# Score, selection and recurrence products over 128 rows with zeroed halves, in place of 64- and 4-row products, in a two-block transformer kernel

## The reference

```python
s = (einsum('bqhd,bkhd->bhqk', qn, k_nope) + einsum('bqhr,bkr->bhqk', qr, k_rope)) * ATTN_SCALE
```

```python
s = einsum('bhcqd,bhckd->bhcqk', q_blk, k)          # c = 0, 1; d = 64
p = softmax(where(mask, s, -inf)); a = p[:, :, 0] - lam * p[:, :, 1]
```

```python
w = exp(D - m) * einsum('bhcjd,bhcsd->bhcjs', q, k); h = einsum(w, v) / max(|w.sum|, exp(-m))
```

## Time and profile before

| | us |
|---|---|
| median of 3 runs | 2067.62 |
| lowest, highest | 2066.59, 2071.74 |
| span of the profiled execution, first to last instruction | 2061.6 |
| TensorE busy in it | 1951.5 (95%) |
| VectorE busy | 879.3 (43%) |
| ScalarE busy | 671.9 (33%) |
| mean granted TensorE clock | 0.985 of full |

### The profile page before, as it was taken

The page is one execution under the profiler, slowest core; times in us unless marked ns, Lnnn a source line. Parts: engine busy times, 40 slices in busy tenths (PEclk is TensorE's granted clock), DMA queues, the critical chain, the costliest instruction groups (busy, mean ns, idle before and its releaser), DMA issues. The chain is left out here.

```text
span 2061.6 us, 36391 instructions
## 1 busy us (share of the span) xinstructions
PE 1951.5 (95%) x16088; PEld 1383.8 (67%) x16088; DVE 879.3 (43%) x1395; ACT 671.9 (33%) x1138; POOL 60.4 (3%) x97
## 2 busy tenths in 40 slices
PE   7999989888999999998889999999999999999998
PEld 5554444445885444444468888878888888887887
DVE  4111111104641111111156656875655665786663
ACT  2000000004440000000054546674545554675552
POOL 0000000000000000000020000010000000011000
PEclk8999999999999999999999999999999999999999
DMA  9999999998669999999966545336545555425551
GB/s 409 399 426 426 426 426 426 427 425 354 265 251 424 426 428 426 427 426 427 425 284 219 189 168 184 126 126 220 195 172 200 201 184 184 153 96 192 194 194 62
DMA packets 56767, 598.33 MB, mean 290 GB/s; under 512 B 6291, under 2 KB 6803, under 8 KB 9747
## 3 DMA queue, kind: packets, MB, share of 16 engines
q1 hardware_dynamic: 55444, 592.44, 71.9%
q10 hardware_dynamic: 1152, 3.41, 0.6%
HBM read 594.78 MB, written 1.05 MB: 289 GB/s over the span
## 5 line engine op out<-in xcount | busy, mean ns | idle before, releaser
L1978 DVE TENSOR_TENSOR SPLIT<-RING,SPLIT 128x2048 fp32r<-128x2048 f32 (+2 forms) x178 | 398.9, 2256 | 143.7 <-ACT SPLIT L1456 143.5
L758 PE MATMUL PS<-RING,WK 128*32 128x512 f32 x816 | 367.4, 604 | 41.1 <-DVE WK L2247 26.1
L1125 PE MATMUL PS<-HTB,SPLIT 128*128 128x512 f32 x1152 | 404.4, 397 | 0.0
L1456 ACT ACTIVATE SPLIT<-RING 128x2048 fp32r<-128x2048 f32 (+2 forms) x178 | 332.7, 1888 | 49.7 <-DMA RING<-in_units 49.7
L1126 PE MATMUL PS<-HTB,SPLIT 128*128 128x256 f32 x1152 | 321.4, 279 | 0.0
L758 PEld LDWEIGHTS PS<-RING,WK 128*32 128x32 f32 x816 | 86.8, 111 | 284.6 <-issue 249.6
L1125 PEld LDWEIGHTS PS<-HTB,SPLIT 128*128 128x128 f32 x1152 | 216.2, 188 | 51.7
L1604 ACT ACTIVATE WK<-PS 128x128 f32<-128x128 f32 x64 | 17.8, 278 | 691.8 <-PE PS L724 691.8
L1126 PEld LDWEIGHTS PS<-HTB,SPLIT 128*128 128x128 f32 x1152 | 216.9, 188 | 0.2
L724 PE MATMUL PS<-RING,WK 128*32 128x128 f32 x5696 | 185.7, 276 | 6.7 <-issue 6.5
L724 PEld LDWEIGHTS PS<-RING,WK 128*32 128x32 f32 x5696 | 162.2, 110 | 29.8 <-issue 27.5
(11 more groups left out here) (341 smaller groups left out, 2344.7 us busy)
## 6 DMA issues: line engine op xcount, KB each, us to landing
RING<-in_units SPq DMA_DIRECT2D x171, 1024.0 KB, 4.8
RING<-in_w_down SPq DMA_DIRECT2D x53, 2048.0 KB, 32.6
RING<-in_w_gate SPq DMA_DIRECT2D x45, 2048.0 KB, 30.6
RING<-in_w_up SPq DMA_DIRECT2D x44, 2048.0 KB, 34.1
WK<-in_w_up SPq DMA_DIRECT2D x17, 2048.0 KB, 34.6
WK<-in_w_gate SPq DMA_DIRECT2D x16, 2048.0 KB, 33.6
WK<-in_w_down SPq DMA_DIRECT2D x6, 2048.0 KB, 36.8
SEAT<-in_w_up SPq DMA_DIRECT2D x3, 2048.0 KB, 27.8
```

The lines of the kernel that those rows point to most:

```text
L758: t = pe.matmul(PS[32 * i:32 * i + 32, 4 + h, :], mo.HE[:, pb, 32 * f:32 * f + 32], v[:, c, 512 * h:512 * h + 512], start=f == 0, stop=f == 3)
L1125: pe.matmul(out.rearrange("p (z b n) -> p z b n", z=2, b=2), wh, HTB[:, :, :, c, :], start=start, stop=False)
L1456: ac.activation(unit_part(u, 0), loaded(u), ACT.Copy).then_inc(s_hi, 1)
L1978: dv.tensor_tensor(unit_part(u, 1), loaded(u), unit_part(u, 0).bitcast(F32), ALU.subtract).then_inc(s_lo, 1)
```

## The change

- `ml.KR` (256 columns) becomes `ml.KZ`, two copies of 256 columns: copy 0 has the rotated key on partitions 0 to 63 and zeros below, copy 1 the reverse. `scores(h)` takes all 128 rows of `ml.QR` and copy h mod 2.
- `mx.DK` becomes `mx.KZ`, two heads in turn, each with two such copies, for d = 0 and 1.
- `mx.MM` is cleared on all 128 partitions, and the selection product runs over 128 rows.
- The convolved queries go by silu from `mx.CO` into the halves of `mx.KZ` (which the scores have left by then), two half-row instructions for each query channel; the keys stay in place.
- POOL clears `ml.KZ` at the start of mla, and `mx.KZ` and `mx.MM` at the start of each mixer, after the previous stage's last product. VectorE waits for that.
- For keys, VectorE multiplies by the cosine in place in `TQ`, and so first waits for the swap product that reads `TQ`; then it adds twice, once per half.

```diff
-        ml.KR = al(256)
+        ml.KZ = al(512).rearrange("p (z n) -> p z n", z=2)
-        mx.DK = al(1024).rearrange("p (h n) -> p h n", h=4)
+        mx.KZ = al(1024).rearrange("p (k z n) -> p k z n", k=2, z=2)
@@ POOL, mla
+                    po.memset(ml.KZ, 0.0).then_inc(s_mh, 1)
@@ POOL, mixer
+                    po.wait_ge(s_unit, UNIT[stage])
+                    for v in (mx.KZ, mx.MM):
+                        po.memset(v, 0.0).then_inc(s_mh, 1)
@@ TensorE, mla scores
-                    pe.matmul(o, ml.QR[dp:dp + 64, pr, i * 128:i * 128 + 128], ml.KR[dp:dp + 64, 0:m], start=False,
+                    pe.matmul(o, ml.QR[:, pr, i * 128:i * 128 + 128], ml.KZ[:, h % 2, 0:m], start=False,
@@ TensorE, decays
-                pe.matmul(PS[:, 6, 0:256], cs("sel")[0:4, h * 128:h * 128 + 128], mx.MM[0:4, :], start=True, stop=True)
+                pe.matmul(PS[:, 6, 0:256], cs("sel")[:, h * 128:h * 128 + 128], mx.MM, start=True, stop=True)
...
-                    pe.wait_ge(s_cos, 4 * l + 4)
-                k, q = mx.CO[dp:dp + 64, 2 * ch + 1, :], mx.CO[dp:dp + 64, 2 * ch, :]
+                    pe.wait_ge(s_cos, 6 * l + 6)
+                k, q = mx.CO[:, 2 * ch + 1, :], mx.KZ[:, ch, h % 2, :]
@@ TensorE, differential scores
-                        t = pe.matmul(o, mx.DQ[64 * d:64 * d + 64, h, i * 128:i * 128 + 128],
-                                      mx.DK[64 * d:64 * d + 64, h, 0:128 + 128 * i], start=True, stop=True)
+                        t = pe.matmul(o, mx.DQ[:, h, i * 128:i * 128 + 128], mx.KZ[:, h % 2, d, 0:128 + 128 * i],
+                                      start=True, stop=True)
@@ ScalarE
-                    ac.activation(mx.CO[:, i, :], mx.CO[:, i, :], ACT.Silu).then_inc(s_cos, 1)
+                    if i % 2:
+                        ac.activation(mx.CO[:, i, :], mx.CO[:, i, :], ACT.Silu).then_inc(s_cos, 1)
+                        continue
+                    for z in range(2):
+                        half = slice(64 * z, 64 * z + 64)
+                        ac.activation(mx.KZ[half, i // 2, z, :], mx.CO[half, i, :], ACT.Silu).then_inc(s_cos, 1)
@@ VectorE, key of mla
-                dv.tensor_tensor(ml.KR, ml.TQ[:, 0, :], cos, ALU.mult).then_inc(own.up(), 1)
                 dv.wait_ge(s_latp, 1)
+                dv.tensor_tensor(ml.TQ[:, 0, :], ml.TQ[:, 0, :], cos, ALU.mult).then_inc(own.up(), 1)
...
-                dv.tensor_tensor(ml.KR, ml.KR, ml.R2, ALU.add).then_inc(s_latv, 1)
+                dv.wait_ge(s_mh, 2)
+                dv.tensor_tensor(ml.KZ[0:64, 0, :], ml.TQ[0:64, 0, :], ml.R2[0:64, :], ALU.add).then_inc(own.up(), 1)
+                dv.tensor_tensor(ml.KZ[64:128, 1, :], ml.TQ[64:128, 0, :], ml.R2[64:128, :], ALU.add).then_inc(s_latv, 1)
@@ VectorE, rotate of the mixer
-                    dst = (mx.DK if i % 2 else mx.DQ)[:, i // 2, :]
+                    h, tq = i // 2, mx.TQ[:, i % 3, :]
                     dv.wait_ge(s_tq, 4 + 8 * l + i + 1)
-                    dv.tensor_tensor(dst, mx.TQ[:, i % 3, :], cos, ALU.mult).then_inc(own.up(), 1)
+                    dst = tq if i % 2 else mx.DQ[:, h, :]
+                    if i % 2:
+                        dv.wait_ge(s_sw, 4 + 8 * l + i + 1)
+                    dv.tensor_tensor(dst, tq, cos, ALU.mult).then_inc(own.up(), 1)
...
+                    dv.wait_ge(s_mh, 6 + 2 * l)
+                    if h >= 2:
+                        dv.wait_ge(s_sc, 16 + 8 * l + 2 * (h - 2) + 2)
+                    dv.tensor_tensor(mx.KZ[0:64, h % 2, 0, :], tq[0:64, :], mx.R2[0:64, :], ALU.add).then_inc(own.up(), 1)
+                    dv.tensor_tensor(mx.KZ[64:128, h % 2, 1, :], tq[64:128, :], mx.R2[64:128, :], ALU.add).then_inc(s_qr, 1)
```

More of the change, by code:

```diff
@@ L997, in scores @@
             def scores(h):
-                bk, pr, dp = h % 2, h // 2, 64 * (h % 2)
+                bk, pr = h % 2, h // 2
                 pe.wait_ge(s_lata, 11 + h // 2)
@@ L1259, in decays @@
             def decays(h):
-                dp, ch = 64 * (h % 2), h // 2
+                ch = h // 2
                 if h:
@@ L1265, in decays @@
                     pe.wait_ge(s_pm, 8 + 8 * l + 8)
-                pe.matmul(PS[:, 6, 0:256], cs("sel")[0:4, h * 128:h * 128 + 128], mx.MM[0:4, :], start=True, stop=True)
-                pe.matmul(PS[:, 6, 256:384], cs("sel")[0:4, h * 128:h * 128 + 128], mx.MM[0:4, 128:256], start=True,
+                pe.matmul(PS[:, 6, 0:256], cs("sel")[:, h * 128:h * 128 + 128], mx.MM, start=True, stop=True)
+                pe.matmul(PS[:, 6, 256:384], cs("sel")[:, h * 128:h * 128 + 128], mx.MM[:, 128:256], start=True,
                           stop=True).then_inc(s_mdm, 1)
@@ L1869, in sums @@
                                (s_nsq, 8 * l + 2 * h + b + 1))
-                ac.wait_ge(s_mh, 3)
+                ac.wait_ge(s_mh, 4)
                 for z in range(2):
@@ L2503, in rotate @@
                     settle()
-                    dv.tensor_tensor(dst, dst, mx.R2, ALU.add).then_inc(s_qr, 1)
+                    if i % 2 == 0:
+                        dv.tensor_tensor(dst, dst, mx.R2, ALU.add).then_inc(s_qr, 1)
+                        return
+                    dv.wait_ge(s_mh, 6 + 2 * l)
[3 more added lines that the diff above has]
+                    dv.tensor_tensor(mx.KZ[64:128, h % 2, 1, :], tq[64:128, :], mx.R2[64:128, :], ALU.add).then_inc(s_qr, 1)
                 def scores(h):
```

## The result

The kernel after took 2071.97 us (median of 13 runs, 2068.60 to 2075.38), the kernel before 2065.73 beside it (13 runs, 2061.97 to 2071.74): ratio 1.0026, 95% interval 1.0019 to 1.0033. That is 5.4 us slower by the ratio, at the edge of what I had called no change. I had forecast 2070.1. The profiled spans are 2068.9 and 2061.6, so +7.3 for +2.5.

A forecast was written before the change was run, and what follows sets the result against it. It took VectorE as the mixers' bound, VectorE and ScalarE as the latent attention's cycle, the weight stream in the second expert layer. -1.2 +3.7 = +2.5 us: span 2061.6 to 2064.1, plus 6.0 for the median: 2070.1 us, range 2060 to 2074.5.

The forecast's parts named there:

- its own case: Whole kernel: the main forecast, 2070.1 us, own range 2067 to 2073, given a 57% chance.
- TensorE's prices: TensorE alone: latent attention head 1.30 us instead of 2.09, decay calls 0.59 less, differential score calls 0.24 more; sum -9.1.
- Latent attention: Head loop: only VectorE's waits for score products shrink, -1.2 of TensorE's 6.3 us; cycle then 3.25 us.
- Its -1.2 passed on: Expert layer behind the latent attention: begins its stream 1.2 us earlier, so the span keeps -1.2; bounds 0 and -6.3.
- Mixers, rotations: VectorE in each mixer: one more half-row add per odd rotation, 0.34 us each, delays growing to +1.58 us.
- Silus: ScalarE in each mixer: six silus instead of four take 0.65 us more, ending 2.24 us later than before.
- Bounds: VectorE in the mixers: an added half-row add costs between 0.17 us (half) and 0.43 us (full duration).
- 1 (TensorE bounds everything): Whole kernel: TensorE is the bound everywhere and every row-mode change saved pays; -9.1 us, 2058.5 us, chance 12%.
- 2: Rival on the mixers: VectorE's delay is covered and TensorE's own balance arrives; -4.0 us, 2063.6 us, chance 16%.
- 3, the ring: Mixers: odd rotations wait for swap products, those for longer score calls, those for rotations; +6.9 us, 2074.5 us, chance 12%.
- 4: Rival on TensorE: the row-mode drains don't go by row count and stay; 2071.3 us, chance 3%.
- Clears and waits: POOL's clears, 1.5 us per mixer and 0.6 in latent attention, stay hidden; nothing queued behind the new waits is delayed further.

The follow-up runs named there:

- scores64: Kernel after with only the differential score products back on 64 rows, half-row adds kept; 2071.35 us median, ratio 1.0021 to the kernel before.
- wide: Kernel after with its half-row adds and half-row silus widened to 128 rows, same count; 2068.57 us median, ratio 1.0010 to the kernel before.
- after again: The kernel after, unchanged, in a second profiled execution; span 2068.3 us.
- mla_sel: Kernel before with only the latent attention's part and the mixers' selection products over 128 rows; 2064.59 us median, ratio 0.9994.
- recur4: Kernel after with only the recurrence's query products back on 64 rows, so four silus, not six; 2069.18 us median, ratio 1.0013 to the kernel before.
- late4: mla_sel with 4 more filler products ahead of the expert layer behind the latent attention; run once, no median given, +3.77 us in that layer.
- warm7: mla_sel with 7 filler products for 4 in the expert layer's routing; 2063.02 us median, once more 2063.49, ratio to the kernel before 0.9983 both times.
- mla_only: Kernel before with only the latent attention's part of the change, mixers untouched; 2064.03 us median, ratio 0.9986.

## Why the prediction was right, and where its size was off

The median 2071.97 lies 1.9 above the forecast, inside its range and its own case. That it is so near is in part luck. The change was forecast at +2.5 and came at +5.4 by the ratio; the span was forecast at 2064.1 and came at 2068.9, 4.8 above. The 6.0 that I added to the span for the median rested on 3 runs of the kernel before (2067.62, and 2065.73 in the 13 beside the result); in the kernel after the median stands 3.1 above the span. The two errors, +4.8 and -2.9, cancel to 1.9. By its steps:

- **TensorE's prices: right.** A head at 1.31, decay calls 0.65 + 0.66, score calls +0.24. The overlap of the 64-row pairs is real and was worth 0.3 of the mixer's 3.1 (scores64), 0.24 a call on TensorE.
- **Latent attention: right.** -1.35 for -1.2, all of it in the two waits of VectorE that I named, cycle 3.25.
- **Its -1.2 passed on: wrong.** "I pass -1.2 on" held only with seven fillers. I had read the clock at 1.00 in the stream and the mixer and not looked at it in the routing between, where it was 0.57 under the fillers. The terms cancel: 0.04 net in that part of the trace, not -1.2.
- **Mixers, rotations: place right, size off.** The term "full step 0.34" for a half-row add measured 0.44, and the step behind the second 0.46. An odd rotation grew by (1307.46-1305.77)-(1304.42-1303.29) = 0.56, not 0.34. The silus started 1330.97-1327.36 = 3.61 late, of which 1.18 was brought into the mixer (1.59-1.35+1.39-0.45): +2.43, where I had +1.59. The third score call waited 1.22 for rotation 5, where I had about 1.
- **Silus: size off.** "Six take 0.65 more", by a step of 0.33: they took 2.38-1.24 = 1.14 more. Together +3.57 at their end, where I had +2.24; the first query-key product waited 1.57 for them, where I had 1. The mixer ends at +3.13, so 0.44 came back behind the silus, where I had 0.38 (0.55 at the sums less 0.17): the two mis-sized terms are the whole difference.
- **Bounds.** 0.17 and 0.43 for a half-row add: the upper end was below the measured 0.44 to 0.46. A row that I passed over said it, the gates' pair of 4-row operations of the kernel before, reading rows 0 to 3 and then 32 to 35: 0.51 from start to start at 0.47 each, while a full-row one of the same kind and length stepped 0.40.

```profile
1275.33 0.47 DVE L2627 TENSOR_SCALAR WK<-PS,VE 4x256 f32<-4x256 f32 x1 [1.95 <-PE PS L596]
1275.84 0.47 DVE L2628 TENSOR_SCALAR WK<-PS,VE 4x256 f32<-4x256 f32 x1
...
1335.71 0.48 DVE L2574 TENSOR_SCALAR WK<-PS,WK 128x256 f32<-128x256 f32 x1
1336.11 0.34 DVE L2576 TENSOR_SCALAR WK<-PS,WK 128x128 f32<-128x128 f32 x1
```

- **Rivals.** 1 (TensorE bounds everything) fell: 9.9 us less on TensorE, slower. 2 fell: the VectorE delay isn't covered. 3, the ring: it needs rotations 5 and 7 to wait for their swap products, and in the kernel after their cosine multiplies (1305.77 and 1314.72) follow without idle time; the longer score calls, without which there is no ring, are worth only 0.3 (scores64). There is no ring, and its 6.9 is near the +7.3 of the spans by accident. 4: the drains went.
- **Clears and waits:** right, 1.21 of POOL's time with nothing behind it. The key rotation cost nothing to speak of: the kernel after is 1.51 late at 515 us, ahead of it, and 1.59 at 546.

The sum as measured: -1.35 + 1.39 + 3.13 + 2.99 = +6.2, against 5.4 by the ratio (3.9 to 6.8).

## What to carry to other kernels

When work is moved from an engine with the larger busy share to one with the smaller, read first which of them the waits name, then price the added operations by the start of the next one, in the way they will stand (which rows, behind what), not by their duration. And when a stage is made shorter, look at the granted clock of the stages behind it: a wait that the slow clock used to fill may become idle time that makes the next products slow, and a few filler products can keep the gain.

## What was not expected of the hardware

**An operation that starts at other rows doesn't overlap its neighbour.** So far as the traces go, it is not the number of rows that counts but where they start. On ScalarE in the kernel after, a half-row silu on rows 0 to 63 behind a full one starts 0.32 behind it (1331.85, 1332.17), as full ones do behind each other; the second half and the full one behind it come 0.43 to 0.44 each (0.88 and 0.86 for two). In the kernel before a 4-row one on ScalarE, starting at row 0, let the next start after 0.33:

```profile
1278.52 0.42 ACT L1889 ACTIVATE WK<-WK 4x256 f32<-4x256 f32 x1
1278.85 0.36 ACT L1808 ACTIVATE WK<-PS 128x256 f32<-128x256 f32 x1
```

On VectorE both steps around the second half are 0.44 to 0.46, with the same columns and waits as in wide, where they are 0.34. The Trainium skill has this for VectorE ("VectorE: DVE Perf Modes", section on two Vector instructions with no wait between them): an instruction whose input or output starts in another group of 32 rows than the last one's starts only when all earlier ones have finished. The trace agrees, 0.44 and 0.46 against 0.34, on the second half-row add and on what follows it; an estimate by that rule, read beforehand, with the duration 0.42 for each of the two steps, would have put the rotation's extra at 0.34+0.08+0.08 = 0.50 at least, where 0.56 was measured and 0.34 forecast. That ScalarE does the same is what its steps here suggest; two half-row operations that both start at row 0 would settle it and weren't tried.

**The clock in a short routing stretch.** Behind an idle 1.74 us TensorE ran at the lower level in all seven executions that had it (after, after again, wide, mla_sel, recur4, scores64, late4), and behind 0.45 in neither warm7. mla_only is the exception: it fell on the fillers and again on the expert products, with 0.41 idle between.

Why does a latent attention that ends 1.35 earlier keep the clock up under the fillers, some 10 us later? The clock's records of the 14 traces give most of an answer, if each fall is counted from the clock's first fall in the same execution (at 31.92 us in the kernel before, where the stretch from 31 to 32 us has a mean clock of 0.96, and the one from 605 to 606 has 0.68, so the fall there is at 605.36; 33.83 and 610.68 in the kernel after). Then the fall near this layer stands at 573.44 in all four executions with the old latent attention and at 576.85 in all eight that have the new one and four fillers; mla_only has one more, at 570.03. The places are the same in all, and the work moves past them. Counted in the same way the fillers begin at 573.29 to 573.85 with the old latent attention, so the fall stands at the end of the 40-column products; with the new one they begin at 570.46 to 572.65, and ahead of 573.44 TensorE was at the fillers. In mla_only, at 570.68, the earlier place stands at the end of the 40-column products; but scores64, at 570.46, had no fall there, and why the one and not the other stays open. Two things follow for the experiments. warm7 (once more, 571.79) and mla_sel (571.77) stand at the same place and differ in the fillers alone: 0.44 idle behind them and no fall, 1.74 and the later fall (mla_only, with 0.41, has part of its fillers at the lower clock and isn't explained by this). And late4, at 572.65, fell short of the 573.29 where the old kernels begin: it doesn't test whether the fall comes on the fillers again when the layer is moved back to that place.
